# Two transformer blocks in float32 on one core: ScalarE's table load, the first weight unit and the vectors at the program's begin

## The reference

```
h = x + rms_norm(merged(rms_norm(x) * g @ w_in) @ w_out)      # attention, conformer convolution, gates
h = h + rms_norm((silu(gate) * up) @ w_down)                  # gate, up = split(rms_norm(h) @ w_gate_up)
x = layer_norm(ALPHA * h + even_layer(h))                     # stick-breaking attention, pooling
x = layer_norm(ALPHA * x + odd_layer(x))                      # RWKV-7 with a state scan over the tokens
```

## Time and profile before

| | us |
|---|---|
| median of 3 runs | 2488.95 (2487.85 to 2489.44) |
| profiled execution, its own time | 2488.02 |
| its span | 2486.2 |
| TensorE busy | 2436.4 (98%) |
| VectorE busy | 1606.6 (65%) |
| ScalarE busy | 1187.5 (48%) |
| GpSimd busy | 75.6 (3%) |
| mean granted TensorE clock | 0.996 of 2.4 GHz |

### The profile page before, as it was taken

One profiled execution on the slowest core, in us unless ns is written; L12 is line 12 of the kernel. 1 busy time (PEld: TensorE's weight loads), 2 busy tenths in 40 slices (PEclk: granted clock), 3 DMA queues, 4 the chain that ended last, 5 costly groups with the idle time before them and its releaser, 6 DMA issues.

```text
span 2486.2 us, 38025 instructions
## 1 busy us (share of the span) xinstructions
PE 2436.4 (98%) x15334; PEld 2101.1 (85%) x15334; DVE 1606.6 (65%) x2159; ACT 1187.5 (48%) x1565; POOL 75.6 (3%) x98
## 2 busy tenths in 40 slices
PE   8999999999999999999999999999999999999997
PEld 7888888888888888888888788888787888887776
DVE  6889888875766666665444756676721676755566
ACT  5444554654544444444444455654546302455644
POOL 0000000000000000000000000000000201021000
PEclk9999999999999999999999999999999999999999
DMA  6665556565465665656655555455733456522463
GB/s 231 191 192 164 161 176 196 184 199 186 128 201 183 192 193 182 195 182 198 190 190 179 158 175 175 160 177 188 232 111 104 144 167 199 175 86 78 128 202 128
DMA packets 419887, 427.68 MB, mean 172 GB/s; under 512 B 25392, under 2 KB 414512, under 8 KB 418880
## 3 DMA queue, kind: packets, MB, share of 16 engines
q1 hardware_dynamic: 414880, 403.07, 51.2%
q0 software_dynamic: 4832, 22.19, 2.9%
HBM read 415.19 MB, written 9.96 MB: 171 GB/s over the span
## 4 chain that ended last, share of the span: by engine, by line
PE 89%; DVE 6%; ACT 3%; issue 1%; DMA 1%; SPq 0%; ACTq 0%; DVEq 0%
PE GP L1949 82%; PE SB L1949 7%; DVE wL L1100 1%; ACT wH L548 1%; DVE y L1100 1%; DVE j L1100 1%; DVE x L1100 0%; DVE f L1106 0%; PE SB L1953 0%; ACT x L865 0%; DMA raw<-w_in_dram 0%; DMA raw<-w_o_dram 0%; DVE sq L1100 0%; DVE wide L1100 0%; DVE xB L1100 0%
## 5 line engine op out<-in xcount | busy, mean ns | idle before, releaser
L1100 DVE TENSOR_TENSOR wL<-raw,wH 128x1024 fp32r<-128x1024 f32 x680 | 825.1, 1225 | 475.7 <-ACT wH L548 474.5
L548 ACT CAST wH<-raw 128x1024 fp32r<-128x1024 f32 x680 | 701.4, 1046 | 493.9 <-PE GP L1949 361.9
L1949 PE MATMUL GP<-u2B,wH 128*128 128x512 f32 x1408 | 442.2, 395 | 0.0
L1949 PE MATMUL GP<-uB,wH 128*128 128x512 f32 x1152 | 363.0, 396 | 0.0
L1949 PEld LDWEIGHTS GP<-u2B,wL 128*128 128x128 f32 x1408 | 264.1, 188 | 65.3 <-DVE u2B L1106 2.1
L1949 PE MATMUL GP<-u2B,wL 128*128 128x256 f32 x1408 | 277.8, 279 | 1.5 <-DVE u2B L1106 1.5
L1949 PEld LDWEIGHTS GP<-uB,wL 128*128 128x128 f32 x1152 | 216.2, 189 | 54.7 <-DVE wL L1100 3.9
L1949 PE MATMUL GP<-xB,wH 128*128 128x512 f32 x768 | 241.2, 395 | 0.0
L1949 PE MATMUL GP<-uB,wL 128*128 128x256 f32 x1152 | 232.1, 283 | 4.1 <-DVE wL L1100 3.2
L1949 PE MATMUL GP<-hB,wH 128*128 128x512 f32 x704 | 221.1, 395 | 0.0
L1949 PEld LDWEIGHTS GP<-u2B,wH 128*128 128x128 f32 x1408 | 214.4, 189 | 0.0
(11 more groups left out here) (415 smaller groups left out, 3131.5 us busy)
## 6 DMA issues: line engine op xcount, KB each, us to landing
raw<-w_gate_up_dram SPq DMA_DIRECT2D x352, 256.0 KB, 3.8
raw<-w_in_dram SPq DMA_DIRECT2D x288, 256.0 KB, 3.4
raw<-ev_w_in_dram SPq DMA_DIRECT2D x192, 256.0 KB, 3.4
raw<-w_down_dram SPq DMA_DIRECT2D x176, 256.0 KB, 3.4
raw<-w_out_dram SPq DMA_DIRECT2D x64, 256.0 KB, 3.6
raw<-ev_w_out_dram SPq DMA_DIRECT2D x64, 256.0 KB, 3.5
dw<-w_k_dram SPq DMA_DIRECT2D x64, 256.0 KB, 3.4
dw<-w_r_dram SPq DMA_DIRECT2D x64, 256.0 KB, 3.3
```

Of the source, the lines that this page charges most:

```text
L548: e.copy(wH[SLOT[i]], raw[k].rearrange("p (k n) -> p k n", k=4)).then_inc(s["hi"], 1)
L1100: return e.tensor_tensor(o, a, b, op)
L1949: return e.matmul(o, l, r, start=start, stop=stop, skip_group_check=True)
```

## The change

ScalarE gets an explicit load of the table set `sqrt_and_others` as its first instruction. Unit 0 is split right behind activation tile 0, on ScalarE (cast) and VectorE (subtraction); tiles 1 to 3 follow. vec is transferred in two parts: columns 0 to 255 first as before, columns 256 to 615 between x chunk 2 and unit 2, with a semaphore of its own, `vecs`, for which ScalarE waits ahead of tile 4, VectorE ahead of uL tile 4, and GpSimd ahead of cst. Nothing is computed otherwise.

```diff
--- before.py
+++ after.py
@@ -283,7 +283,7 @@
 SUMMED = {"p1": 0, "p2": 6, "l1": 0, "l2": 8}
 
 
-SEMS = """vec xc0 xc1 xc2 xc3 cst bias raw0 raw1 raw2 raw3 raw4 hi lo unit lh ev eva val dr0 dr1 dr2 dr3 th tl
+SEMS = """vec vecs xc0 xc1 xc2 xc3 cst bias raw0 raw1 raw2 raw3 raw4 hi lo unit lh ev eva val dr0 dr1 dr2 dr3 th tl
 sq1 st1 rt1 rs1 filled z ga aw cv at_vt at_vc at_pe at_act at_dve cn_pe cn_act cn_dve c_h c_l mg mh ml
 p1_sq p1_st p1_rt p1_f h1 sq2 st2 rt2 rs2 silu hm hh hl p2_sq p2_st p2_rt p2_f h2
 cnt wp0 wp1 sk_vt sk_vc sk_pe sk_act sk_dve xm_h xm_l pw pp pm pmx_h pmx_l
@@ -500,7 +500,7 @@
 
 
         def sync_program(e):
-            e.dma_start(vec, d["vec"]).then_inc(s["vec"], 16)
+            e.dma_start(vec[:, 0:256], d["vec"][:, 0:256]).then_inc(s["vec"], 16)
             def x_chunk(i):
                 e.dma_start(x[:, 4 * i:4 * i + 4, :], d["xT"][:, 4 * i:4 * i + 4, :]).then_inc(s[f"xc{i}"], 16)
 
@@ -527,6 +527,8 @@
                                 d[name][sl // 2, 2 * ku + j].rearrange("p (k n) -> p k n", k=2)[:, :, cols]).then_inc(done, 16)
                 if i < 3:
                     x_chunk(i + 1)
+                if i == 1:
+                    e.dma_start(vec[:, 256:NVEC], d["vec"][:, 256:NVEC]).then_inc(s["vecs"], 16)
             for lo, hi in ((0, 4), (4, 8), (8, 12), (12, 14), (14, 16)):
                 e.wait_ge(s["x2"], hi)
                 e.dma_start(out[:, lo:hi, :], x2[:, lo:hi, :]).then_inc(s["out"], 16)
@@ -534,18 +536,21 @@
 
         def scalar_program(e):
             def split(u):
-                for i in range(SPLIT[u - 1] if u else 0, SPLIT[u]):
-                    if W0 <= i < WS:
-                        continue
-                    m = NTH[i]
-                    k, uses, _ = LANDING[m]
-                    e.wait_ge(s[f"raw{k}"], 32 * uses)
-                    if PRIOR[i] >= 0:
-                        e.wait_ge(s["unit"], PRIOR[i] + 1)
-                    if SLOT[i] == RING - 1 and PRIOR[i] < W1 <= i:
-                        e.wait_ge(s["jp2"], BASE[2][-1][0])
-                        e.wait_ge(s["jd2"], BASE[2][-1][2])
-                    e.copy(wH[SLOT[i]], raw[k].rearrange("p (k n) -> p k n", k=4)).then_inc(s["hi"], 1)
+                for i in range(SPLIT[u - 1] if u else 1, SPLIT[u]):
+                    one(i)
+
+            def one(i):
+                if W0 <= i < WS:
+                    return
+                m = NTH[i]
+                k, uses, _ = LANDING[m]
+                e.wait_ge(s[f"raw{k}"], 32 * uses)
+                if PRIOR[i] >= 0:
+                    e.wait_ge(s["unit"], PRIOR[i] + 1)
+                if SLOT[i] == RING - 1 and PRIOR[i] < W1 <= i:
+                    e.wait_ge(s["jp2"], BASE[2][-1][0])
+                    e.wait_ge(s["jd2"], BASE[2][-1][2])
+                e.copy(wH[SLOT[i]], raw[k].rearrange("p (k n) -> p k n", k=4)).then_inc(s["hi"], 1)
 
             def around_split(name, tile, first):
                 def tiles(u):
@@ -613,6 +618,8 @@
                         e.wait_ge(s["vec"], 16)
                     if i % 4 == 0:
                         e.wait_ge(s[f"xc{i // 4}"], 16)
+                    if i == 4:
+                        e.wait_ge(s["vecs"], 16)
                     e.activation(uH[:, i, :], x[:, i, :], ACT.Copy, scale=V("g_pre", i)).then_inc(s["th"], 1)
 
             def empty_in(n, sl, j):
@@ -1067,7 +1074,10 @@
                      "kk": kk(), "decay": decay(), "solve": solve(), "gate": gate()}
             chains = [chain(k) for k in range(3)]
 
-            for i in range(4):
+            e.preload_act_table_set("sqrt_and_others")
+            u_tile(0)
+            one(0)
+            for i in range(1, 4):
                 u_tile(i)
             stream("w_in", empty_in, lambda u: [u_tile(i) for i in tile_range(u, 4)])
             stream("w_attn_o", empty_ao)
@@ -1106,13 +1116,16 @@
                 return e.scalar_tensor_tensor(out=o, in0=a, scalar=s_, in1=b, op0=op0, op1=op1)
 
             def split(u):
-                for i in range(SPLIT[u - 1] if u else 0, SPLIT[u]):
-                    if W0 <= i < WS:
-                        continue
-                    m = NTH[i]
-                    e.wait_ge(s["hi"], m + 1)
-                    tt(wL[SLOT[i]], raw[LANDING[m][0]].rearrange("p (k n) -> p k n", k=4), wH[SLOT[i]].bitcast(F32),
-                       ALU.subtract).then_inc(s["lo"], 1)
+                for i in range(SPLIT[u - 1] if u else 1, SPLIT[u]):
+                    one(i)
+
+            def one(i):
+                if W0 <= i < WS:
+                    return
+                m = NTH[i]
+                e.wait_ge(s["hi"], m + 1)
+                tt(wL[SLOT[i]], raw[LANDING[m][0]].rearrange("p (k n) -> p k n", k=4), wH[SLOT[i]].bitcast(F32),
+                   ALU.subtract).then_inc(s["lo"], 1)
 
             def ahead_of_split(name, tile, first):
                 def tiles(u):
@@ -1173,6 +1186,8 @@
                         e.wait_ge(s["vec"], 16)
                     if i % 4 == 1:
                         e.wait_ge(s[f"xc{i // 4}"], 16)
+                    if i == 5:
+                        e.wait_ge(s["vecs"], 16)
                     stt(uL[:, i - 1, :], x[:, i - 1, :], V("g_pre", i - 1), uH[:, i - 1, :].bitcast(F32),
                         ALU.mult, ALU.subtract).then_inc(s["tl"], 1)
 
@@ -1757,7 +1772,10 @@
                      "halves": halves(), "zero": zero(), "lora1": lora1(), "kk": kk(), "decay": decay(), "solve": solve(), "gate": gate()}
             chains = [chain(k) for k in range(3)]
 
-            for i in range(5):
+            for i in range(2):
+                u_tile(i)
+            one(0)
+            for i in range(2, 5):
                 u_tile(i)
             stream("w_in", empty_in, lambda u: [u_tile(i) for i in tile_range(u, 5)])
             stream("w_attn_o", empty_ao)
```

## The result

| | before | with the change |
|---|---|---|
| median of 20 runs, us | 2488.76 (2486.94 to 2491.06) | 2492.39 (2489.08 to 2495.41) |
| profiled execution, its own time | 2488.02 | 2492.27 |
| its span | 2486.2 | 2490.4 |
| TensorE busy | 2436.4 | 2438.3 |
| VectorE busy | 1606.6 | 1606.1 |

The ratio is 1.0015, with a 95% interval of 1.0008 to 1.0021: a loss of 2 to 5 us. Forecast was 1.6 us less, with a range up to 2490.1. Two executions behind this document, one of the run with vec split (2692.74 us) and one of the kernel before, taken beside a later set of runs (5804.01 us), were far slower than all others and are left out of the ratios.

The account below looks back on a forecast made before the run. TensorE, 98% busy, bounds the kernel through the wait ending at 21.17 us. Earlier first wL 0.6, cst's move the rest, second load and longer SP program 0: -1.6 us, from 2488.95 to 2487.3, range 2484.9 to 2490.1.

Parts of the forecast that it names:

- The question: What decides is when TensorE gets past the wait ending at 21.17 us, not when its first real matmul starts.
- Table load, second load: Load moved to the begin: x chunk 0 to first ACTIVATE 1.37 to about 0.07 us; second load at 33.88 goes, worth 0.
- vec in two: At the begin, 180 KB less ahead of x and units 0 and 1: 0.4 us earlier; unit 2 still at 12.87.
- Unit 0 behind one tile: First GP matmul at 9.5 instead of 11.51 us, 2.0 earlier; only 0.6 of it on the path, through the buffers.
- cst goes behind: cst issued near 12.3 instead of 9.13, mostly behind units 3 and 4: unit 4 no longer waits 1.6 us; low bound 0.6.
- Rival A: TensorE's clock falls at the longer stand ahead of 19.55 us, price 1.8 us; total 2489.2 to 2490.2; chance 0.13.
- Rival B: vec's tail costs more than its bytes, by its added issue of about 0.6 us; gain 1.0, time 2487.9; chance 0.10.
- D: cst late: TensorE's sum of squares waits if cst is over 8.7 us in flight instead of 6.5; chance 0.03.

Follow-up runs that it names:

- vec whole: The change with vec in one transfer and no `vecs`, keeping the early table load and unit 0 behind one tile; 2489.13 us, ratio 1.0004 against the kernel before.
- table load alone: The kernel before plus only the table load ahead of all waits; 2490.78 us, ratio 1.0005.
- tiles ahead: vec whole, plus activation tiles 4 to 7 ahead of the splits of units 3 and 4, squares one unit earlier; 2487.48 us, on another chip 2485.09.
- start filled: The kernel with the tiles ahead, with seven warm-up matmul calls on vec instead of five; 2483.85 us, ratio 0.9979 against the kernel before.
- moved tiles but nothing of the change: The kernel before with only activation tiles 4 to 7 ahead of the splits of units 3 and 4 and earlier squares; 2488.03 us, ratio 0.9996.
- tail last: The change with vec's tail issued behind x chunk 3, waited for ahead of tile 8, cst issued ahead of its wait; 2490.81 us, ratio 1.0011 against before.
- tail first: The change with vec's tail issued right behind its head, ahead of x chunk 0; 2489.95 us, ratio 1.0005 against the kernel before.
- bytes added: The kernel before, with vec's last 360 columns transferred a second time between x chunk 2 and unit 2; 2489.06 us, ratio 1.0000.
- stand filled: The change plus six more warm-up matmul calls just ahead of TensorE's wait for uL 6; 2489.60 us, ratio 1.0002 against the kernel before.
- cst early: The change, but GpSimd issues cst after x chunk 1 and waits for vec's tail only behind that; 2491.31 us, ratio 1.0009 against the kernel before.
- split of vec alone: The kernel before plus only vec's transfer in two parts and the three waits for `vecs`; 2491.40 us, ratio 1.0010.

## Why the prediction was wrong

- *The question was right.* TensorE's time is set where it gets past the wait for uL 6 and by the clock behind it. An early first matmul alone gained nothing (vec whole, table load alone), and removing that wait gained (tiles ahead, start filled).
- *Table load, second load.* As written: at 0.74 us, and none near 34. It freed x chunk 0 to the first ACTIVATE. Worth 0 by itself: the wait for uL 6 takes it back.
- *vec in two: the step that failed.* "I take 0.4: the weights land at 6 to 8 us, where bytes do limit", and "these have the same bytes ahead as before and land as before, 12.87". Unit 2 was cast at 14.46, and everything behind it was later by the same 1.6 us. The three other kernels with these transfers have unit 2 at 14.12, 13.82 and 13.51, so the change's profile is the latest of four; the kernel before, the one with the table load alone and the one with moved tiles but nothing of the change have 12.87 to 13.00. I had the row (182 GB/s at 4 to 6 us) and used it only as a bound on the gain. It says that the queues had room there, so that the bytes taken out had cost little or nothing and would cost wherever else they went. Measured one by one, the tail's place (tail last) and the extra issue (tail first) cost unit 4 0.6 and 0.4 us, and both together (bytes added) 0.8; SP's added issue was entered at 0.
- *Unit 0 behind one tile.* First GP matmul at 10.57, not 9.5: only unit 0's landing was off (8.21 for 7.2); cast and subtraction took what the rows said. That landing belongs to the one execution: in the change with the stand filled, with the same transfers, unit 0 was cast at 7.27 and the first GP matmul came at 9.63. Not foreseen was that the warm-up matmuls, which wait for vec, also start earlier (2.90 instead of 3.66) and end at 7.15, so that the first stand was 3.42 us and not 1.6.
- *cst goes behind: the second step that failed.* Forecast: 1.6 us that unit 4 no longer waits. vec's tail landed near 13.1, not 12; cst went out at 13.39, and unit 4 only at 13.75 and 14.33, since unit 1's subtraction ended at 13.69 and not 12.15. So cst travelled beside unit 4, not behind it. Unit 4 was cast at 20.02 instead of 16.8. The term is 0, not 1.6: from unit 2's cast to unit 4's it was 5.56 us in the change, 5.49 with cst early and 5.53 before. What did move by the forecast 1.6 us is unit 3: with cst early it is cast 4.17 us behind unit 2 and unit 4 another 1.32 behind it, in the change 2.60 and 2.96. This is as if cst's bytes had gone from ahead of unit 3 to ahead of unit 4, and the wait hangs on unit 4.
- *Rival A came true* and is the larger part. Its price of 1.8 was 1.68 in the profile. I gave it 0.13, because a forecast stand of 2.5 us was "still under the 3.21"; the stand became 3.66, from 19.11 to 22.77 where the forecast had 17.0 to 19.55, and the clock also fell at stands of 1.79 and 2.67. A and late data are one case, not two: what makes unit 4 late also lengthens the stand. Their sum, +1.6 and +1.7, was in none of my cases.
- *Rival B* was right in kind (the added issue is not hidden) and was priced at a gain of 1.0. The other estimate there, from the table of the Trainium skill (DMA: Bandwidth & Descriptors, Bandwidth), was 1.3 us for the 180 KB, 0.85 more than by bytes. The bytes added put units 2 and 4 back by 0.8 in all, 0.35 more than by bytes, and tail first, at 0.4 us, shows that an issue alone accounts for that. So the trace does not bear out an extra price for the transfer's size. The table of the Trainium skill is of transfers issued from GpSimd; SP issues this one.
- *D* did not occur: no wait for cst, even at 13.39.
- Open: the landing of unit 1 (11.37 in the change, 11.04 in its copy with the stand filled, 10.4 to 10.9 in the other four with a split). That the head alone does this was not tried. Nor is it known how much of unit 2's 1.6 us in the change's profile is that one execution's: bytes and issue account for 0.8.

The balance, by medians: late data 0.8 us (change with the stand filled, 2489.60, against 2488.76; 1.1 against the 2488.46 measured beside it), lower clock 2.8 us (2492.39 against 2489.60), together 3.6. These are differences between sets of runs on different chips, where the kernel before itself had medians of 2488.46 to 2488.93, so each is good to about half a microsecond to one. That the larger share is the clock's rests on the pair with and without the filled stand and on the granted clocks of their executions.

## What to carry to other kernels

Before a transfer is put off to let others pass, see whether the queues are full where it lies: where they have room it may be free, as it was here, and it costs wherever they are full. Before a start is made earlier, find the next wait of the same engine and see what it hangs on; unless that moves too, the gain becomes a longer stand, and on TensorE a longer stand can lower the clock and cost more than was won. A few matmuls into a scratch bank, placed in a stand that can't be removed, give that back.

## What the runs showed of the hardware

- With the stand ahead of uL 6 at 1.79 us (split of vec alone), 2.67 (table load alone) and 3.66 us (the change) a stretch at 0.50 came, and with stands of 2.70, 3.20 and 3.44 us (tail first, tail last, cst early) none came in the profiled executions. So the length of one stand doesn't decide alone, and the same kernel's executions differ: the change's 20 runs spread over 6.3 us, the 11 with the stand filled over 3.1.
- The granted clock at the head of a trace can't always be read. In the second run with the tiles ahead the window from 10.4 to 15 us (below, behind two rows of TensorE's timeline) gives 1.00, but a wL pair takes 0.63 us there, as in the 0.50 stretch of the earlier trace rows, instead of 0.39:

```profile
11.77 0.63 PE L1964 MATMUL GP<-uB,wL 128*128 128x256 f32 x2
12.20 1.05 PE L1964 MATMUL GP<-uB,wH 128*128 128x512 f32 x2
```
```profile
10.40:15.00 4.60, 4.60 (x19) 4.03 (x20) 3.05 (x5) 2.90 (x5) 0.00 (x0) 1.00 1.05 409
```

  The five warm-up calls had not raised the clock for that execution, and so the first three steps, up to 13.5 us, ran slow. With seven, the profiled execution ran at full steps from its first unit (0.70, from 11.21 to 11.90 us).
- An issue of SP takes a different time from one execution to the next: the tail of vec, eighth in the same sequence, took it 0.87, 0.59, 0.49 and 0.43 us in four kernels, and 0.42 when it was second of all; x chunk 2, with the same transfers ahead of it in five kernels, took 0.60 to 1.06.
